# Gate and up weights of the experts in another channel order, with the tile transposes, scale and shift to match

## The reference, cut to what matters

```python
h = modulate(rms_norm(x, norm_ffn_g[l]), sh2, sc2)      # h * (1 + sc2) + sh2, per channel
a = silu(einsum('td,edf->tef', h, w_gate)) * einsum('td,edf->tef', h, w_up)
y = einsum('tef,efd->td', a * gates[:, :, None], w_down)  # gates: two experts per token
x = x + g2 * y
```

## Time and profile before

| | us |
|---|---|
| runs shown, median of 3 | 1656.82 |
| the profiled execution's own time | 1653.37 |
| its span | 1651.5 |
| PE busy in it | 1540.9 |
| DVE, ACT, POOL busy | 818.6, 269.4, 245.6 |

### The profile page before, as it was taken

One profiled execution on the slowest core, in us unless ns is written; L12 is line 12 of the kernel. 1 busy time (PEld: TensorE's weight loads), 2 busy tenths in 40 slices (PEclk: granted clock), 3 DMA queues, 4 the chain that ended last, 5 costly groups with the idle time before them and its releaser, 6 DMA issues.

```text
span 1651.5 us, 17355 instructions
## 1 busy us (share of the span) xinstructions
PE 1540.9 (93%) x5589; PEld 843.6 (51%) x5590; DVE 818.6 (50%) x1580; ACT 269.4 (16%) x530; POOL 245.6 (15%) x412
## 2 busy tenths in 40 slices
PE   5989999998999999999979999998899899999991
PEld 3774544447885444444434343444588444444440
DVE  2463587663425222233227898999543622322323
ACT  3300000000112211111132000022231211111112
POOL 2000000000000132232210000303000122322220
PEclk9999999999999999999999999999899999999996
DMA  9645047643124978899475454464111799678846
GB/s 337 206 138 171 26 153 236 213 150 127 41 88 181 362 221 266 239 283 291 89 214 157 122 141 116 124 154 105 47 52 77 278 353 345 184 202 264 254 89 229
DMA packets 201458, 302.40 MB, mean 183 GB/s; under 512 B 10517, under 2 KB 160113, under 8 KB 201408
## 3 DMA queue, kind: packets, MB, share of 16 engines
q1 hardware_dynamic: 179040, 222.71, 42.2%
q0 software_dynamic: 18800, 65.39, 15.6%
q10 hardware_dynamic: 3568, 13.63, 2.1%
HBM read 248.55 MB, written 53.10 MB: 183 GB/s over the span
## 4 chain that ended last, share of the span: by engine, by line
PE 78%; DVE 13%; DMA 4%; issue 2%; ACT 1%; POOL 0%; SPq 0%; DVEq 0%; POOLq 0%; ACTq 0%
PE bank L1153 20%; PE bank L1004 20%; PE bank L1083 16%; PE bank L1168 11%; DVE R L1789 5%; PE bank L1135 3%; DVE WX L1364 3%; PE bank L1265 2%; PE bank L987 1%; PE bank L1021 1%; DMA WX<-in_moe_w_gate 1%; DVE R L1341 1%; DMA xsum_scratch<-R,TCUR 1%; PE bank L974 1%; DMA WX<-xsum_scratch 1%
## 5 line engine op out<-in xcount | busy, mean ns | idle before, releaser
L1004 PE MATMUL bank<-HTR,WX 128*128 128x512 f32 x1024 | 453.0, 599 | 5.8 <-DMA WX<-in_hyb_w_in 4.8
L1153 PE MATMUL bank<-WX,R 128*128 x784 | 344.8, 593 | 4.4 <-issue 2.3
L1004 PEld LDWEIGHTS bank<-HTR,WX 128*128 128x128 f32 x1024 | 192.8, 191 | 245.2 <-issue 238.5
L1789 DVE SCALAR_TENSOR_TENSOR R<-R,PT 128x512 f32<-128x512 f32 (+18 forms) x288 | 231.3, 803 | 10.2
L1083 PE MATMUL bank<-WX,R 128*128 128x256 f32 x1024 | 230.8, 384 | 2.2 <-DVE R L1341 1.1
L1153 PEld LDWEIGHTS bank<-WX,R 128*128 128x128 f32 x784 | 145.2, 190 | 168.8 <-issue 168.8
L1341 DVE TENSOR_TENSOR R<-bank,R 128x256 f32<-128x256 f32 (+2 forms) x77 | 38.8, 504 | 373.6 <-ACT R L758 262.5
L1083 PEld LDWEIGHTS bank<-WX,R 128*128 128x128 f32 x1024 | 194.5, 192 | 31.6 <-issue 2.7
L1168 PE MATMUL bank<-WX,R 128*128 x408 | 183.7, 593 | 4.1 <-DVE R L1606 4.1
L1364 DVE SCALAR_TENSOR_TENSOR WX<-WX,CAB 128x256 f32<-128x256 f32 x280 | 135.8, 485 | 10.0
L1617 DVE SCALAR_TENSOR_TENSOR R<-bank,GSLOT,HTR 128x512 f32<-128x512 f32 x51 | 38.3, 751 | 154.0 <-DMA xsum_scratch<-R,TSUM 88.8
(11 more groups left out here) (214 smaller groups left out, 1080.8 us busy)
## 6 DMA issues: line engine op xcount, KB each, us to landing
WX<-in_ada_w SPq DMA_DIRECT2D x48, 1024.0 KB, 11.8
WX<-in_moe_w_gate SPq DMA_DIRECT2D x32, 1024.0 KB, 7.0
WX<-in_moe_w_up SPq DMA_DIRECT2D x32, 1024.0 KB, 12.0
WX<-in_moe_w_down SPq DMA_DIRECT2D x32, 1024.0 KB, 15.1
WX<-in_conf_w SPq DMA_DIRECT2D x20, 1024.0 KB, 9.5
WX<-glu_scratch SPq DMA_DIRECT2D x64, 260.0 KB, 4.4
WX<-in_hyb_w_in SPq DMA_DIRECT2D x10, 1024.0 KB, 12.0
xsum_scratch<-WX ACTq DMA_DIRECT2D x8, 1024.0 KB, 4.2
```

The lines of the kernel that those rows point to most:

```text
L1004: ins = pe.matmul(dst[:], lhs(k), rhs(k), start=(k == 0), stop=(k == kc - 1))
L1153: ins = pe.matmul(M[0][:], XT[:, k, :], WX[:, bass.ds(at + k * 2 * FE, 2 * FE)], start=(k == 0), stop=(k == KC - 1))
L1789: link(dve.scalar_tensor_tensor(out=o[:, t0:HT], in0=p[:, HT * h + t0 - d:HT * h + HT - d], scalar=tap(CTAPS - 1 - d), in1=o[:, t0:HT], op ...
```

## The change

Gate and up weights are read as d = 8 p + k: partition p holds channels 8p to 8p + 7, which are 8 KB side by side in DRAM (8 rows of 256 fp32). They land in WX as two blocks of 2048 elements, gate then up, each (k, f), where before gate and up of one k stood side by side. The gate/up matmul of slice k reads two runs of 256 columns that lie 2048 elements apart. So that the same channels meet, the transpose of slice k takes channels k, k + 8, k + 16, ... of XG, and the scale and shift of the evictions come from a new table MCT in that order. MCT is made once, in layer 0's output projection: ACT stores MC's rows 2 and 3 of both layers to a DRAM scratch and loads them back in the other order, and ACT and DVE wait for mc_in before the first tile's eviction. The down weights, the router and the mixing parts stay.

```diff
--- before.py
+++ after.py
@@ -170,6 +170,7 @@
         IOTAB = sb("IOTAB", [P, P], BF16)
         TOKI = sb("TOKI", [P, MAXT], U32)
         TCUR = sb("TCUR", [P, 1], U32)
+        MCT = sb("MCT", [P, NL, 2, KC])
         TSUM = sb("TSUM", [P, 1], U32)
         SPARE = sb("SPARE", [P, 1])
         RT = sb("RT", [1, 2 * MAXT], I32)
@@ -228,6 +229,8 @@
 
         XG = R[:, 1, 0:D]
         XT = R[:, 1, D:2 * D].rearrange("p (k t) -> p k t", k=KC)
+        XGT = XG.rearrange("p (q k) -> p k q", k=KC)
+        WXP = WX[:, 0:NEB * EXP].rearrange("p (r k f) -> p r k f", k=KC, f=FE)
         YS = R[:, 1, 2 * D:3 * D]
         YL = R[:, 0, 0:D]
         SG = R[:, 1, 3 * D:3 * D + FE]
@@ -275,6 +278,7 @@
 
 
         xn_dram = nc.dram_tensor("xn_scratch", (T + P, D), F32, kind="Internal").ap()
+        mc_dram = nc.dram_tensor("moe_scale_shift_scratch", (NL, 2, D), F32, kind="Internal").ap()
         xs_dram = nc.dram_tensor("xsum_scratch", (T + P, D), F32, kind="Internal").ap()
         g_dram = nc.dram_tensor("gate_scratch", (4, D), F32, kind="Internal").ap()
         glu_dram = nc.dram_tensor("glu_scratch", (D, PADC + T), F32, kind="Internal").ap()
@@ -302,6 +306,8 @@
         brow_out = [sem(f"gate_row_stored{n}") for n in range(NBROW)]
         zeroed = sem("scratch_rows_zeroed")
         rms_sd = sem("rms_root_ready")
+        mc_out = sem("moe_scale_shift_stored")
+        mc_in = sem("moe_scale_shift_by_row_group")
         xn_ok = sem("xn_ready")
         xn_out = [sem(f"xn_stored{n}") for n in range(2)]
         tr = sem("xn_transposed")
@@ -449,18 +455,17 @@
 
             def expert(l, e, b):
 
-                g = i["moe_w_gate"][l].rearrange("e (k p) f -> e p k f", p=P)
-                u = i["moe_w_up"][l].rearrange("e (k p) f -> e p k f", p=P)
+                g = i["moe_w_gate"][l].rearrange("e (p k) f -> e p k f", p=P)
+                u = i["moe_w_up"][l].rearrange("e (p k) f -> e p k f", p=P)
                 dw = i["moe_w_down"][l].rearrange("e (k p) n -> e p k n", p=P)
                 at = b * EXP
-                wgu = WX[:, at:at + 2 * KC * FE].rearrange("p (k n) -> p k n", k=KC)
                 wd = WX[:, at + 2 * KC * FE:at + EXP].rearrange("p (k n) -> p k n", k=2)
                 s = e_in[l][b]
 
                 def pick(w):
                     return w[e] if isinstance(e, int) else w[bass.ds(e, 1)].rearrange("e p k n -> (e p) k n")
-                sp.dma_start(wgu[:, :, 0:FE], pick(g)).then_inc(s, 16)
-                sp.dma_start(wgu[:, :, FE:2 * FE], pick(u)).then_inc(s, 16)
+                sp.dma_start(WXP[:, 3 * b, :, :], pick(g)).then_inc(s, 16)
+                sp.dma_start(WXP[:, 3 * b + 1, :, :], pick(u)).then_inc(s, 16)
                 sp.dma_start(wd, pick(dw)).then_inc(s, 16)
 
             def experts(l):
@@ -747,8 +752,9 @@
                     act.wait_ge(xtr[l], n_tr)
                     for k in range(4):
                         ins = act.activation(XT[:, k, :], TB_[0][:, k * P:(k + 1) * P], ACT.Identity,
-                                             bias=MC[:, l, 3, k:k + 1], scale=MC[:, l, 2, k:k + 1])
+                                             bias=MCT[:, l, 1, k:k + 1], scale=MCT[:, l, 0, k:k + 1])
                     ins.then_inc(xt_a[l], 1)
+                act.wait_ge(mc_in, 16)
                 evict_tile(1)
                 act.wait_ge(tab_ok, l + 1)
                 nt = act.value_load(RT[0:1, 0:1], min_val=1, max_val=MOST)
@@ -765,6 +771,15 @@
             def x_pieces(l, g0, beside=lambda p, j: None):
 
                 for p in range(4):
+                    if (l, p) == (0, 2):
+                        act.wait_ge(ada_fin, NADA)
+                        for n in range(NL):
+                            act.dma_start(mc_dram[n].rearrange("s (k p) -> p s k", p=P), MC[:, n, 2:4, :],
+                                          allow_slow_non_contiguous=True).then_inc(mc_out, 16)
+                    if (l, p) == (0, 3):
+                        act.wait_ge(mc_out, 16 * NL)
+                        act.dma_start(MCT[:].rearrange("p l s k -> p (l s) k"),
+                                      mc_dram.rearrange("l s (p k) -> p (l s) k", p=P)).then_inc(mc_in, 16)
                     for j in range(4):
                         beside(p, j)
                         q = 16 * l + 4 * p + j
@@ -1133,7 +1148,7 @@
                     pe.wait_ge(xg_in[l], n_in)
                     for k in range(KC):
                         ins = pe.transpose(TB_[k // 4][:, P * (k % 4):P * (k % 4) + P],
-                                           XG[:, P * k:P * k + P], IDENT[:])
+                                           XGT[:, k, :], IDENT[:])
                     ins.then_inc(xtr[l], 1)
                 def expert_of(t):
 
@@ -1142,15 +1157,17 @@
                 def buffer_at(e):
 
                     return (e & (NEB - 1)) * EXP
+
+                hid = M[0][:].rearrange("p (g f) -> p g f", g=2)
 
                 def gate_up(t, e):
                     pe.wait_ge(xt_a[l], t + 1)
                     pe.wait_ge(xt_d[l], t + 1)
                     for b in range(NEB):
                         pe.wait_ge(e_in[l][b], ((e + (NEB - b)) >> 2) * 48)
-                    at = buffer_at(e)
+                    at = (e & (NEB - 1)) * 3
                     for k in range(KC):
-                        ins = pe.matmul(M[0][:], XT[:, k, :], WX[:, bass.ds(at + k * 2 * FE, 2 * FE)],
+                        ins = pe.matmul(hid, XT[:, k, :], WXP[:, bass.ds(at, 2), k, :],
                                         start=(k == 0), stop=(k == KC - 1))
                     ins.then_inc(gu[l], 1)
 
@@ -1176,8 +1193,7 @@
                     pe.wait_ge(xt_d[l], 1)
                     pe.wait_ge(e_in[l][0], 48)
                     for k in range(KC):
-                        ins = pe.matmul(M[0][:], XT[:, k, :], W[:, k * 2 * FE:(k + 1) * 2 * FE],
-                                        start=(k == 0), stop=(k == KC - 1))
+                        ins = pe.matmul(hid, XT[:, k, :], WXP[:, 0:2, k, :], start=(k == 0), stop=(k == KC - 1))
                     ins.then_inc(gu[l], 1)
 
                 keep_warm(3)
@@ -1582,9 +1598,10 @@
                     dve.wait_ge(xtr[l], n_tr)
                     for k in range(4, KC):
                         ins = dve.tensor_scalar(XT[:, k, :], TB_[1][:, (k - 4) * P:(k - 3) * P],
-                                                MC[:, l, 2, k:k + 1], MC[:, l, 3, k:k + 1],
+                                                MCT[:, l, 0, k:k + 1], MCT[:, l, 1, k:k + 1],
                                                 ALU.mult, ALU.add)
                     ins.then_inc(xt_d[l], 1)
+                dve.wait_ge(mc_in, 16)
                 evict_tile(1)
                 dve.sem_inc(ys_d[l], 1)
                 dve.wait_ge(gt_ps, l + 1)
```

## The result

16 executions of each kernel, side by side: before 1654.63 us (1651.04 to 1658.86), after 1659.39 us (1656.07 to 1663.66), ratio 1.0028 [1.0019, 1.0038]. The change costs 4.8 us, 0.28%, which is just inside the 0.3% that I had called no change. The forecast was 1697 us: far too much, and for a reason that did not come true.

The account below looks back on a forecast made before the run. PE was taken as the bound, busy 1540.9 of 1651.5 us. 1653.37 + 0 + 0 + 0 + 41 (stepped transposes) = 1694, brought to the median 1697 us; range 1652 to 1712.

Parts of the forecast that it names:

- rival (a): Tile transposes: stepped weight loads stay hidden under 110 ns, below 0.85 ns per column; 1653 to 1660 us; chance 0.35.
- part 1: Two gate/up weight loads per expert in 8 KB runs: 0 us, beside PE; bounds -3 and +24 us.
- part 4: Tile transposes reading XG at a 32-byte step: 0.77 us per tile, 53 tiles, +41 us; bounds 0 and +72 us.
- reading (c): Transposes' weight loads: each new place costs 1.72 ns, as on DVE, so 220 ns per load, +41 us; chance 0.45.
- Its test: Transposes in the changed kernel's tile: LDWEIGHTS longer but below 195 ns with the period unchanged means the loads are hidden.
- late-gathers rival: Tile gathers: rows wait for longer weight packets, +2.2 us per gather, half a microsecond on 49 tiles, +24 us; chance 0.05.
- 1.95 us of slack: Steady tile: POOL sees the gather landed 1.95 us before the transposes that need it start.
- five waits, 2.5 us: PE's weight loads waited 2.5 us in all for tile gathers; taken as the most a faster load could win.
- Packets: DMA transfers of the whole kernel: packets under 2 KB fall by 65,000 whatever the time does.
- Part 2: Gate/up matmuls with the moving operand in two blocks of 256 columns: 0 us; bounds 0 and 3 us.
- Part 3: Scale and shift stored and reloaded by ACT in layer 0's output projection: 0 us; bounds 0 and +10 us.

Follow-up runs that it names:

- e2: Changed kernel's channel order, stepped transposes and table, but weights loaded in 1 KB runs into the old interleaved buffer: 1655.47 us, ratio 1.0003 to the kernel before.
- e3: Changed kernel's 8 KB runs and two blocks, but plain transposes and no table, so channels are mismatched: 1659.59 us, ratio 1.0025 to the kernel before.
- e9: Kernel before plus two idle-filling matmuls behind a layer's first hidden transposes, loads not held back: 1652.23 us, ratio 0.9987.
- e4: Changed kernel plus idle-filling matmuls, one before a layer's second transposes, two behind its first hidden transposes: 1658.63 us, ratio 1.0027 to the kernel before.
- e10: Kernel before, unchanged, profiled once more: one execution, 1658.35 us.
- e11: Changed kernel, nothing altered, profiled once more: one execution, 1657.28 us.
- e1: Changed kernel, but SP issues expert 2's loads only when the layer's second gather has landed: 1654.74 us, ratio 1.0001 to the kernel before.
- e7: Changed kernel with each gate and up load cut into two transfers of 4 KB per partition: 1655.91 us, ratio 1.0000 to the kernel before.
- e12: Changed kernel, 8 KB runs kept, SP paced: expert 1's down weights and expert 2 wait for DVE's first eviction, expert 3 for first gate/up: 1654.9 us, ratio 0.9999.
- e8: Kernel before with a tile's eight transposes at steps 1 to 8 and a layer's first gate/up moving at steps 1 to 8: one execution, 1669.43 us.

## Why the prediction was wrong

- **The range.** The measured 1659.4 lies in it only because it was drawn to take in rival (a). That is luck: the 4.8 us over the kernel before came from part 1, not from part 4.
- **Part 4, the deciding term: wrong.** The step that failed is reading (c), "1.72 ns is what one access to a new place costs whoever asks". It carried DVE's pace over to a weight load, supported by a coincidence of two rates. Measured: 190 ns for the load, thus 190 - 84 = 106 ns of loading proper, 0.83 ns per column, against 57 ns side by side. That is under the 110 ns between two transposes, so reading (a) held, just inside its own limit of 0.85. Forecast +41 us, measured 0.3 to 0.5 (the steady parts of both layers are 0.30 us longer in e2, 0.45 in after). Its test had been named in advance (190 is below 195, period unchanged). The Trainium skill's rule (SBUF — State Buffer, Door 1: The DMA port swizzle), read as half the bandwidth, gave 114 ns of loading proper and 1.5 us, and the runs are near that reading at step 8: 106 ns. They don't agree with its free steps up to 4: the stationary side pays in full at step 2 (194 ns), and the moving one at step 4 (1074 against 592).
- **Part 1, the loads: 0 was wrong, its upper bound was right.** The 8 KB runs are the loss: e3, without steps and table, 1.0025. The late-gathers rival had the mechanism (a row of the gather waits for one weight packet) and had it at 0.05. It forecast +2.2 us per gather; the profiles show +1.3 to 1.4 for gather 2 of layer 0, and +0.5 in layer 1 (means of the table above). It put the loss on 49 tiles and forecast 24 us. In the steady loop the DMA engines are at 0.75 to 0.80, not full, and the 1.95 us of slack cover the rest; only at the two layer starts, where experts 1 to 3 are loaded while the second and third gather run, are they full (1.01 from 541 to 551 us, 1.07 in before) with next to no slack: before's gather 2 had 0.2 us to spare in layer 0, and PE waited 0.48 us for it in layer 1. The question left out was: is there a stretch where the queue is always full and a gather has no slack? The earlier trace rows held five waits, 2.5 us; I read them as something to win.
- **Packets.** 60,880 fewer under 2 KB, against the 65,000 forecast; the saving in DMA time is real and lies beside PE, as said.
- **Part 2, two blocks: right.** 16 products in 6.87 us before and after.
- **Part 3, scale and shift by row group: right at 0.** ACT's timeline in after:

```profile
455.74 1.32 ACTq L777 DMA_DIRECT2D moe_scale_shift_scratch<-MC  x2
...
460.45 0.60 ACT L787 ACTIVATE HTR<-bank 128x512 f32<-128x512 f32 x1 [3.14 <-PE bank L1036]
...
488.17 0.37 ACTq L781 DMA_DIRECT2D MCT<-moe_scale_shift_scratch  x1
...
493.12 0.60 ACT L787 ACTIVATE HTR<-bank 128x512 f32<-128x512 f32 x1 [4.98 <-PE bank L1036]
```

  Idle times of 3.14 and 4.98 where they were 3.15 and 5.04. One size was off: the stores landed after 15.0 us, above my bound of 13; the cover of 31 us held it.
- **The clock.** I had no term for it. It falls at layer starts in both kernels, and kept up by two added matmuls at each layer's start it gives back 0.13% in the kernel before (e9) and nothing in after (e4, 1.0027).

What stays open: how the 4.8 us of the medians come about in single executions. From the first gate/up to the loop's second, both layers together, before and e10 take 44.9 and 49.9 us, after and e11 52.0 and 48.8, so that an unchanged kernel is once slower there than the changed one. That the loss lies there is shown by the medians of e1, e7 and e12, not by the traces. By e4 against e9, both with the clock held, 3.6 us of it are seen. Also open is what part packet length has in e7 and in the loss as a whole, apart from SP's pace.

## What to carry to other kernels

Here a weight load could be stepped at almost no cost as long as its loading proper (106 ns) stayed under the distance between two matmuls (110 ns); take the rate from that engine's own rows, not from another engine's. Longer DMA packets were faster for the transfer and, where the engines were full, slower for the gather that shared them: before lengthening runs, look for the stretch where the engines are full and a small, urgent transfer has no slack, and let the prefetch wait for that transfer (one semaphore wait was worth the whole loss here). One pair of profiles is no evidence for a fall of the clock; a second profile of each kernel took away half of that story.

## What was not expected of the hardware

- A weight load of 128 fp32 columns takes 141 ns side by side and 194, 201, 207, 205, 218, 228, 207 ns at steps of 2 to 8 elements (e8; in after 190 at step 8); a moving operand of 512 columns takes 592, 610, 842, 1074, 1074, 1098 ns at steps 1, 2, 3, 4, 6, 8.
- The records of single packets of the weights, at a layer's start: 1 KB 48 to 50 ns, 4 KB 159 to 164, 8 KB 309. So 4 KB already has nearly the rate of 8 KB (25 to 26 against 26.5 bytes per ns), at half the wait for others.
- A gather's first row moves 1.7 to 1.8 us after issue at a layer's first tile, with no weights in transfer, and 4.1 to 4.7 us at the second and third tile in all kernels whose loads weren't held back, whatever the packet length. In e12 it moved after 2.1 us at the second tile, with the DMA engines at 0.95 or more, so that busy engines alone don't explain the delay.
- The granted clock can fall to half behind some 2 us of idle PE, in some executions of the same kernel and not in others.
